# First compression of a two-block transformer: inner layer with its operands swapped, buffers cleared ahead of the last bias row, output weights from the second unit on held behind the bias rows

## The reference

```python
n_c = (S - CMP_BLOCK) // CMP_STRIDE + 1          # (256 - 32) // 16 + 1 = 15
def compress(t, pe, w1, w2):                      # t: (1, 256, 4, 64)
    blk = t[:, tok_idx] + pe[:, None, :]
    blk = jnp.moveaxis(blk, 3, 2).reshape(B, n_c, N_KV, CMP_BLOCK * HEAD_DIM)   # 60 rows of 2048
    return jax.nn.gelu(blk @ w1) @ w2             # w1: 2048 x 256, w2: 256 x 64
k_cmp = compress(kvh(kc), pe_k, w1_k, w2_k)
v_cmp = compress(kvh(vc), pe_v, w1_v, w2_v)
...
s = jnp.einsum('bsgrd,bngd->bgrsn', q, k_cmp).astype(jnp.float32) * scale
p, denom, _ = masked_softmax(s + bias_c, dist_c >= 0)
p_cmp = p / jnp.maximum(denom, 1e-30)
o_cmp = jnp.einsum('bgrsn,bngd->bsgrd', p_cmp, v_cmp.astype(jnp.float32))
```

## Time and profile before

| | |
|---|---|
| times of three runs | 1333.7, 1336.67, 1336.89 us; median 1336.67 us |
| the profiled execution | 1335.29 us, of which the span of the instructions is 1333.5 us |
| PE, PEld, DVE, ACT, POOL busy | 97%, 81%, 62%, 49%, 19% of the span |
| mean granted clock of TensorE | 0.996 of full speed |

### The profile page before, as it was taken

One profiled execution on the slowest core, in us unless ns is written; L12 is line 12 of the kernel. 1 busy time (PEld: TensorE's weight loads), 2 busy tenths in 40 slices (PEclk: granted clock), 3 DMA queues, 4 the chain that ended last, 5 costly groups with the idle time before them and its releaser, 6 DMA issues. The chain is left out here.

```text
span 1333.5 us, 19346 instructions
## 1 busy us (share of the span) xinstructions
PE 1293.8 (97%) x7309; PEld 1083.4 (81%) x7309; DVE 821.3 (62%) x1235; ACT 647.3 (49%) x940; POOL 257.0 (19%) x337
## 2 busy tenths in 40 slices
PE   6998999999999999999999999999999999999997
PEld 5996788888799988888888788888877667888886
DVE  3448765555564477655555755556888777655554
ACT  4328754444453367543444644546543663544442
POOL 5320110000000021102000489601275120200000
PEclk9999999999999999999999999999999999999999
DMA  9980456555455643467755555654535334555551
GB/s 286 259 139 17 145 164 193 188 189 189 158 190 190 159 120 89 162 213 166 234 189 178 168 188 188 220 189 156 188 104 162 119 117 161 197 191 187 184 192 48
DMA packets 155659, 225.82 MB, mean 169 GB/s; under 512 B 13027, under 2 KB 107467, under 8 KB 155596
## 3 DMA queue, kind: packets, MB, share of 16 engines
q1 hardware_dynamic: 141008, 208.36, 49.9%
q0 software_dynamic: 9840, 11.60, 4.3%
q10 hardware_dynamic: 4748, 5.01, 1.2%
HBM read 223.59 MB, written 1.27 MB: 169 GB/s over the span
## 5 line engine op out<-in xcount | busy, mean ns | idle before, releaser
L597 DVE TENSOR_TENSOR units_lo<-raw_units,units_hi 128x2048 fp32r<-128x2048 f32 x96 | 222.1, 2313 | 154.5 <-ACT units_hi L551 154.5
L197 PE MATMUL bank<-units_hi,turned_hi 128*128 128x512 f32 (+1 forms) x792 | 307.0, 388 | 5.3 <-DVE rows L3105 1.8
L180 DVE TENSOR_TENSOR units_lo<-raw_units,units_hi 128x2048 fp32r<-128x2048 f32 (+2 forms) x103 | 233.3, 2273 | 118.0 <-ACT units_hi L172 117.8
L199 PE MATMUL bank<-units_hi,turned_lo 128*128 128x512 f32 (+1 forms) x792 | 302.1, 381 | 0.0
L198 PE MATMUL bank<-units_lo,turned_hi 128*128 128x512 f32 (+1 forms) x792 | 301.8, 381 | 0.0
L172 ACT ACTIVATE units_hi<-raw_units 128x2048 fp32r<-128x2048 f32 (+2 forms) x103 | 193.2, 1886 | 125.1 <-PE bank L199 91.1
L551 ACT ACTIVATE units_hi<-raw_units 128x2048 fp32r<-128x2048 f32 x96 | 183.5, 1912 | 103.7 <-PE bank L199 95.6
L197 PE MATMUL bank<-units_hi,second_hi 128*128 128x512 f32 (+1 forms) x560 | 218.8, 391 | 0.4 <-ACT rows L2277 0.4
L199 PE MATMUL bank<-units_hi,second_lo 128*128 128x512 f32 (+1 forms) x560 | 216.5, 387 | 0.0
L198 PE MATMUL bank<-units_lo,second_hi 128*128 128x512 f32 (+1 forms) x560 | 216.4, 386 | 0.0
L197 PEld LDWEIGHTS bank<-units_hi,turned_hi 128*128 128x128 f32 x792 | 149.1, 188 | 35.8 <-DVE units_lo L180 3.0
(11 more groups left out here) (347 smaller groups left out, 1828.0 us busy)
## 6 DMA issues: line engine op xcount, KB each, us to landing
raw_units<-in_ffn_w_up SPq DMA_DIRECT2D x88, 512.0 KB, 4.7
raw_units<-in_ffn_w_in SPq DMA_DIRECT2D x88, 512.0 KB, 4.7
raw_units<-in_ffn_w_down SPq DMA_DIRECT2D x22, 1024.0 KB, 5.0
raw_units<-in_ffn_w_out SPq DMA_DIRECT2D x22, 1024.0 KB, 5.0
raw_units<-in_w_in SPq DMA_DIRECT2D x18, 1024.0 KB, 5.1
raw_units<-in_b_w_q SPq DMA_DIRECT2D x12, 1024.0 KB, 5.1
raw_units<-in_a_w_in SPq DMA_DIRECT2D x10, 1024.0 KB, 11.1
raw_units<-in_kv_w SPq DMA_DIRECT2D x6, 1024.0 KB, 5.1
```

Of the source, the lines that this page charges most:

```text
L180: dve.tensor_tensor(lo, raw, hi.bitcast(F32), ALU.subtract).then_inc(m.lo_done, 1)
L197: pe.matmul(out, lh, rh, start=start, stop=False, skip_group_check=True)
L199: return pe.matmul(out, ll, rh, start=False, stop=True, skip_group_check=True)
L597: dve.tensor_tensor(m.WL[:, slot(n0 + j), :], m.RAW[:, slot(n0 + j), :], m.WH[:, slot(n0 + j), :].bitcast(F32), ALU.subtract).then_inc(m.l ...
```

## The change

The inner layer is done the other way round: the pieces of the keys (64 columns, of which 60 are used, since each group now has a sixteenth, cleared column) stand still, and the 256 columns of the inner weights stream past. The keys' product goes to partitions 0 to 63 and the values' to partitions 64 to 127 of one bank, in alternation. One gelu then serves both, on 256 columns. Its result has pieces in rows and hidden units in columns, so two transposes follow (`hidden_turn_tensor`) and a copy to `GH`; the second layer of the keys moves behind the first part of unit 9. On POOL, `HID` and `PC` are cleared after fifteen bias rows instead of sixteen. SP waits for all 16 bias rows before it loads unit 12.

```diff
@@ project_a_tensor
     project_gate_a_tensor(pe, m, n + 8)
-    compress_keys_tensor(pe, m)
     ...
     score_pair_a_tensor(pe, m, 0)
-
-    pe.wait_ge(m.s("gelu1_steps"), 1)
+    hidden_turn_tensor(pe, m)
+
     project_keys_a_part(pe, m, n + 9, 4, 0, 0)
+    compress_keys_tensor(pe, m)
+    project_keys_a_part(pe, m, n + 9, 4, 0, 1)
     compress_scores_tensor(pe, m, 0)
-    project_keys_a_part(pe, m, n + 9, 4, 0, 1)
     compress_scores_tensor(pe, m, 1)
@@ project_a_vector
     compress_hidden_vector(dve, m)
+    spread_hidden_vector(dve, m)
     split_lo(dve, m, first_unit("a_out"))
@@ compress_gpsimd
     for n, (dst, src) in enumerate(((m.A.RK, m.A.KC2), (m.A.RV, m.A.VC2))):
+        pool.memset(dst[:, :, :, NCMP:16], 0.0)
         for g in range(KV):
...
-    bias_a_gpsimd(pool, m, range(10, HEADS))
-    pool.wait_ge(m.s("a_products_made"), 2)
+    bias_a_gpsimd(pool, m, range(10, 15))
+    pool.wait_ge(m.s("a_products_made"), 1)
     pool.memset(m.A.HID, 0.0).then_inc(m.s("padding_zero"), 1)
     pool.memset(m.A.PC, 0.0).then_inc(m.s("padding_zero"), 1)
+    bias_a_gpsimd(pool, m, range(15, HEADS))
@@ compress_hidden_tensor
-    for n, (w1, r) in enumerate(((m.A.W1K, m.A.RK), (m.A.W1V, m.A.RV))):
-        pe.wait_ge(m.s("blocks_ready"), n + 1)
-        for u in range(16):
-            for k in range(2):
-                ins = mm(pe, m.pb[4 + n][:, k * 64:k * 64 + KV * NCMP], w1[:, u, k * P:(k + 1) * P],
-                         r[:, u, :, :].rearrange("p g n -> p (g n)"), u == 0 and k == 0, u == 15)
-        ins.then_inc(m.s("a_products_made"), 1)
+    pe.wait_ge(m.s("blocks_ready"), 2)
+    for u in range(16):
+        for n, (w1, r) in enumerate(((m.A.W1K, m.A.RK), (m.A.W1V, m.A.RV))):
+            ins = mm(pe, m.pb[4][n * DH:(n + 1) * DH, 0:S], r[:, u, :, :].rearrange("p g n -> p (g n)"), w1[:, u, :],
+                     u == 0, u == 15)
+    ins.then_inc(m.s("a_products_made"), 1)
+
+def hidden_turn_tensor(pe, m):
+    pe.wait_ge(m.s("gelu0_steps"), 6)
+    for k in range(2):
+        ins = pe.transpose(m.pb[6][:, S + k * P:S + (k + 1) * P], m.A.GX[:, k * P:(k + 1) * P], m.IDENT[:, :])
+    ins.then_inc(m.s("a_products_made"), 1)
@@ compress_hidden_vector, spread_hidden_vector
-    gelu_vector(dve, m, "gelu0", m.A.GX, m.A.GY, hidden(0), m.A.GH[:, :, 0:60])
+    gelu_vector(dve, m, "gelu0", m.A.GX, m.A.GY, m.pb[4][:, 0:S], m.A.GX)
     dve.wait_ge(m.s("a_products_made"), 2)
-    gelu_vector(dve, m, "gelu1", m.A.GX, m.A.GY, hidden(1), m.A.GX)
+    dve.tensor_copy(m.A.GH, m.pb[6][:, S:2 * S].rearrange("p (k n c) -> p k n c", k=2, n=2))\
+        .then_inc(m.s("hidden_copied"), 1)
@@ out_sync
+            if stage == "a_out" and n == first_unit(stage) + 1:
+
+                sp.wait_ge(m.s("bias_a_in"), 16 * HEADS)
```

More of the change, by code:

```diff
@@ L1136, in compress_gpsimd @@
     for n, (dst, src) in enumerate(((m.A.RK, m.A.KC2), (m.A.RV, m.A.VC2))):
+        pool.memset(dst[:, :, :, NCMP:16], 0.0)
         for g in range(KV):
             blocks = bass.AP(src.tensor, src.offset + g * S, [list(src.ap[0]), [2, 16], [16, NCMP]])
-            ins = pool.tensor_tensor(dst[:, :, g, :], blocks,
+            ins = pool.tensor_tensor(dst[:, :, g, 0:NCMP], blocks,
                                      m.PE[:, n, :].unsqueeze(2).to_broadcast([P, 16, NCMP]), ALU.add)
@@ L1228, in compress_keys_scalar @@
     act.wait_ge(m.s("padding_zero"), 1)
-    src = m.pb[6][:, 0:60].rearrange("p (g n) -> p g n", g=KV)
+    src = m.pb[6][:, 0:DH].rearrange("p (g n) -> p g n", g=KV)
     for par in range(2):
         rows = slice(par * DH, (par + 1) * DH)
-        ins = act.activation(m.A.KCB[rows, :, par, 0:NCMP], src[rows, par::2, :], ACT.Copy)
+        ins = act.activation(m.A.KCB[rows, :, par, 0:NCMP], src[rows, par::2, 0:NCMP], ACT.Copy)
     ins.then_inc(m.s("k_cmp_ready"), 1)
-    gelu_scalar(act, m, "gelu1", m.A.GY)
 def compress_weights_scalar(act, m):
@@ L1257, in compress_hidden_vector, with spread_hidden_vector @@
 def compress_hidden_vector(dve, m):
-    def hidden(n):
-        return m.pb[4 + n][:, 0:P].rearrange("p (k c) -> p k c", k=2)[:, :, 0:60]
     dve.wait_ge(m.s("a_products_made"), 1)
-    gelu_vector(dve, m, "gelu0", m.A.GX, m.A.GY, hidden(0), m.A.GH[:, :, 0:60])
-    dve.wait_ge(m.s("gelu0_steps"), 6)
+    gelu_vector(dve, m, "gelu0", m.A.GX, m.A.GY, m.pb[4][:, 0:S], m.A.GX)
     dve.wait_ge(m.s("a_products_made"), 2)
-    gelu_vector(dve, m, "gelu1", m.A.GX, m.A.GY, hidden(1), m.A.GX)
-    dve.wait_ge(m.s("gelu1_steps"), 6)
+    dve.tensor_copy(m.A.GH, m.pb[6][:, S:2 * S].rearrange("p (k n c) -> p k n c", k=2, n=2))\
+        .then_inc(m.s("hidden_copied"), 1)
+def spread_hidden_vector(dve, m):
+    dve.wait_ge(m.s("hidden_copied"), 1)
     dve.wait_ge(m.s("padding_zero"), 3)
     for k in range(2):
-        src = m.A.GX[:, k, :].rearrange("p (g n) -> p g n", g=KV)
+        src = m.A.GH[:, k, 1, :].rearrange("p (g n) -> p g n", g=KV)[:, :, 0:NCMP]
         ins = dve.tensor_copy(m.A.HID[:, k, :, :, 0:NCMP], src.unsqueeze(2).to_broadcast([P, KV, 4, NCMP]))
@@ L3221, in views @@
     A.CD = cut.take(TT, HEADS)
-    A.GX = cut.take(2, 60)
-    A.GY = cut.take(2, 60)
-    A.GH = cut.take(2, 60)
+    A.GX = A.VCR.rearrange("p g d -> p (g d)")
+    A.GY = cut.take(S)
+    A.GH = cut.take(2, 2, DH)
     A.NM = cut.take(NPA, 2, 2)
@@ L3241, in views @@
     cut = Cutter(rows, 0)
-    A.RK = cut.take(16, KV, NCMP)
-    A.RV = cut.take(16, KV, NCMP)
+    A.RK = cut.take(16, KV, 16)
+    A.RV = cut.take(16, KV, 16)
     cut = Cutter(rows, 0)
```

4 lines of the change are left out of this document (2 added, 2 removed).

## The result

The changed kernel took 1327.81 us, median of 5 executions (1327.54 to 1328.18), against 1334.66 us (1333.69 to 1336.89, 5 executions) of the kernel before in the same comparison. The ratio is 0.9946, 95% interval 0.9931 to 0.9960: 6.85 us faster. The profiled execution took 1327.74 us with a span of 1325.3.

What follows compares the result with a forecast made beforehand. PE's queue was taken as the bound, nearly met by POOL and transfers through DVE. 1.57 - 7.3 + 0.3 - 0.29 - 0.57 = -6.3, less 0.2 for bias rows: 1336.67 - 6.1 = 1330.6 us, range 1328.0 to 1334.6.

Steps and rivals of the forecast that it cites:

- the sum: All terms to DVE's third score pair: 6.3 us earlier, cut to 6.1 us faster for the bias rows.
- The start: PE's inner layer waits for POOL's values' pieces, starting at 68.45 us (68.3 to 68.6) instead of 66.88: +1.57 us.
- The inner layer: PE's 64 records in overlapping array halves, 0.21 us per two: 6.9 us against 14.2, -7.3 us.
- rival 1: Array halves overlap only in part; 0.17 us recurs at each of 16 steps, adding 2.5 us: 1333.1 us, chance 0.10.
- The transposes: Two added PE transposes behind the new gelu: +0.3 us, no wait, with 0.2 us to spare.
- The bias rows: Row 15 lands at 83.3 us, row 16 at 89.2, in time for DVE's bias add; +0.2 us laid on.
- From start to third pair: From PE's inner layer start at 68.45 us to DVE taking the third score pair at 100.15: 31.7 us.
- (2) late row 16: The last bias row stays late for DVE's bias add; at 96.5 all gain is lost: 1336.5 us, chance 0.12, all or part.
- (3) no overlap: Array halves don't overlap, weight loads stay hidden: inner layer 13.4 us, change +0.4, 1337.1 us, chance 0.03.
- (4) weight loads exposed: No overlap and each record waits for its weight load: layer 22.1 us, +8.9, 1345.6 us, chance 0.05 with its like.
- The granted clock drops after PE's new idle: Listed sign of being wrong: PE's clock falls after its new 1.6 us idle at 67 us.

Runs made afterwards that it cites:

- no hold: The changed kernel without SP's wait for the bias rows ahead of unit 12: 1336.37 us, ratio 1.0015 to the kernel before.
- late piece: The changed kernel with POOL's issues of bias rows 11 to 13 moved ahead of its eighth addition: 1333.45 us, ratio 0.9994 to the kernel before.
- swap alone: The changed kernel without both side edits (clears behind all 16 bias rows, units 12 and 13 not held back): 1336.01 us, ratio 1.0012.
- side edits alone: The kernel before with its old inner layer, plus clears after 15 bias rows and SP's wait ahead of unit 12: 1333.80 us, ratio 0.9994.

## Why the prediction came out as it did

**The mechanism was right; a term was mis-sized, and most of the distance is the level.** Forecast and result are 2.8 us apart. Of these, 1336.67 - 1334.66 = 2.0 us are the time of the kernel before: I subtracted from a median of three that stood 2.2 us above the 113 executions' 1334.44. The rest, 6.85 - 6.1 = 0.75 us, is the sum. In the profiled pair the sum is further off: DVE took the third pair 7.92 us earlier, not 6.3. Of these 1.6 us, 1.57 are a wait that didn't come and 0.41 are PE's earlier beginning; the layer and the rest took 0.35 back. That the result fell outside the range, by 0.19 us, is also luck: from 1334.44 the same sum gives 1328.3, and all 36 executions of the changed kernel have a median of 1328.93. The half-width that I gave to the scatter (1.6 us) was smaller than the error of the level itself.

**The start: +1.57 us predicted, nothing measured, the step that failed.** "I take the end at 68.45 us" came from one profile, in which POOL began at 62.42. POOL's own 5.86 us were right; the beginning was not a constant. In the 16 profiles of this case POOL begins its pieces between 60.3 and 62.8 us, while the last record of unit 7 ahead of the inner layer starts between 65.6 and 67.1 us, and the two don't move together. In the changed kernel's four profiles PE waited 0, 0.1, 0 and 1.65 us. So the term is a spread from 0 to 1.7, and 3.4 where POOL loses the race with DVE's split; at 1.65 the third pair comes at 99.83 instead of 98.55. I should have given it 0 as its lower bound; I gave 68.3 to 68.6.

**The inner layer: -7.3 predicted, -7.1 measured** (7.09 us against 6.9). Each pair takes 0.22 us where the short group of the earlier trace rows gave 0.21, and nothing recurs at the 16 steps. The share that the Trainium skill's "TensorE: Matmul & The Clock Gate" (Part 3, measured speedup) gives for three tiles, 2.38 of 3, would have meant an estimated 8.5 us; that is 1.6 us above my 6.9, not the 2.5 of rival 1 that the prediction puts beside it. The trace doesn't agree with that share for two tiles: the same 64 records took 13.17 us in one half after the other and 7.09 us alternating, 1.86 times faster including the start of the pipeline.

**The transposes: no wait predicted, 0.22 us measured**, 0.2 and 0.5 us in two other profiles. With the layer over at 73.56 the gelu's copy starts only at 74.63, behind DVE's split of a unit: the layer is over 1.8 us earlier than the 75.35 of the forecast, DVE is free only 1.2 us earlier than its 75.84, and the 0.2 us to spare were used up. I had named this price (a slip of 0.5 costs 0.3).

**The bias rows: +0.2 predicted, nothing measured.** Row 15 landed at 79.3, not 83.3 (of that difference 2.0 us are POOL's earlier start), row 16 was issued at 79.92 and landed 5.3 us later at 85.2, 1.6 us before the bias add. The pace of 1.35 us came from rows of another stretch, rows 5 to 9. The Trainium skill's "DMA: Bandwidth & Descriptors" (Queues, rings and completion order, on arbitration; the prediction names another section) says that a DMA engine takes turns between its queues, packet by packet. The estimate of 2.0 us a row that I drew from it and my 1.35 were both too slow. Without the other queue, rows 13 to 15, issued 0.8 us apart, landed within 1.9 us; with SP's loads beside them they needed 8.1 us, more than twice as long. What the hold is worth is shown: all of the gain (1336.37 us without it).

**From start to third pair:** before 39.59 us, forecast 100.15 - 68.45 = 31.7, measured 32.08 here and 31.93 in the last profile. This part of the sum was good to 0.4 us. The later stages moved as a whole, as predicted.

**The rivals.** (1) partial overlap: not seen. (2) late row 16: not seen. POOL's stand is tied to row 15's landing (79.3, then the issue at 79.92), and rows 13 to 15 are faster alone; the late row came back only without the hold. Its 1336.5 us for a bias add at 96.5 should have been 1336.8 by its own 1 us for 1 us (6.4 lost of 6.3). (3) no overlap: its time, 1334.1 us made on purpose, was right from the true level (1334.44 + 0.4 = 1334.8). (4) weight loads exposed: not seen; even in one half a record took 0.206 us.

**The clock.** "The granted clock drops after PE's new idle" was listed as what would make it wrong. It didn't happen in the result's profile. It does happen in variants: after idle times of 3.4 us (clears behind row 16), 3.4 us (no hold), 4.0 us (late piece) and 4.0 us (swap alone, where PE stands before the values' layer), not after the changed kernel's 1.65. That is a risk that the change brings, since PE now needs the last piece at the start of the layer and not in its middle. The length of the idle time alone doesn't decide it: far ahead of the change, at 16 us, PE stood 1.3 to 2.4 us in eleven of the 16 profiles, of both kernels, and the clock fell to half each time, while in the five with 0.5 us or less it didn't.

**What stays open.** Over four comparisons the changed kernel gained 6.85, 5.54, 4.52 and 3.72 us; all 36 executions give 1328.93 us, 5.5 below before, with 8 above 1332 us (the highest 1335.59), and the first five happened to be at the fast end. PE's start wait, which costs about 1.3 us (third pair 99.83 against 98.55), and a late piece with half a clock (third pair at 103.5 and 104.6 in the two profiles that have it) were both seen or made and would account for such times. No execution lies between 1330.91 and 1332.31 us, as if something happened in those 8 or did not, and the race of POOL's addition with DVE's split is such a thing; but none of the 8 was profiled, so this is argued. Their mean granted clock fits only in part: 0.993 or 0.994 in four of them, lower than in any of the other 28, and 0.995 in the other four, as in thirteen faster ones. What lets the clock fall at 86 to 88 us with PE busy, seen in three profiles of variants (no hold and both with the gate projection first), isn't known.

## What to carry to other kernels

Where two chains end within a microsecond of each other, cost an edit on both: here the swap alone (1336.01 us, a part of it the clock's) and the side edits alone (1333.80) were each worth nothing that could be told, and together 5.5 us. A wait's size, taken from one profile as the difference of two engines' times, has the scatter of both; read it in several executions, or give it 0 as a bound, and subtract from many executions rather than three. When an operation is long in one profile only, look at what the neighbouring engine began just before it. When an edit moves a dependency from the middle of a stage to its start, put independent work of the waiting engine between, as with the gate projection: with the piece made 2.4 us late, the median on one chip was 1330.27 us with it and 1333.45 without.

## What the runs showed of the hardware

- Float32 matmuls into two column halves of the array, alternating, go at 0.22 us for two records of 256 columns for 32 pairs on end; one half alone takes 0.206 us a record.
- An addition of POOL (128x240, 0.72 us) that began 0.08 and 0.15 us after DVE's split of a unit (2.29 us) took 2.79 and 2.76 us; one that began 0.10 us ahead of it took 0.72, and the split 2.76. These are the only two long additions in 16 profiles, and the only two that began behind the split while it had most of its time to run.
- The granted clock fell to half after 3.4 and 4.0 us of idle PE, and at 16 us after 1.3 to 2.4 us, but not after 1.65 us at 67 us. It also fell with PE fully busy, from 86 to 88 us on, for 3.4 to 10 us, in three profiles of variants.
- POOL stands before its 16th bias row until the 15th has landed, and issues it 0.5 to 0.6 us later, at 79.9 us or at 91.5 or 92.0, unless its clears are not over by then.
